# Index key and heads' weights of a sparse-attention indexer: two products or one of 80 columns

## The reference

```python
proj = h @ w_in[l]
q, k, v, ga, iq, ik, iw, xr, gr, ma, mb = jnp.split(proj, offsets, axis=-1)
iq = apply_rope(iq.reshape(B, S, 16, 64), cos_i, sin_i)   # index queries, 16 heads of 64
ik = apply_rope(ik, cos_i, sin_i)                         # one index key of 64
...
iw = iw.astype(jnp.float32) * (IDX_HEADS ** -0.5) * (IDX_DIM ** -0.5)   # one weight per head
dots = jnp.einsum('bqhd,bsd->bqhs', iqb, ik)
idx_score = jnp.einsum('bqh,bqhs->bqs', iwb, jax.nn.relu(dots))
```

## Time and profile before

| | |
|---|---|
| median of 3 runs | 2320.51 us (2318.68 to 2321.33) |
| the profiled execution | 2316.55 us, its span 2314.4 us |
| mean granted clock of the profiled execution | 0.985 |
| PE busy | 2206.8 us, 95% of the span |
| DVE busy | 1760.8 us, 76% |
| ACT busy | 1468.9 us, 63% |
| second block | from about 1540 us of the span to its end |
| heads' weights' products | 1613.5 us and 1985.1 us of the span |

### The profile page before, as it was taken

How to read it: one execution, slowest core, us unless ns; L and a number is a source line. 1 busy time by engine, 2 the same in 40 slices (tenths; PEclk the granted TensorE clock), 3 DMA queues, 4 the chain that set the end, 5 groups by cost and what they waited for, 6 DMA issues and landing times.

```text
span 2314.4 us, 35167 instructions
## 1 busy us (share of the span) xinstructions
PE 2206.8 (95%) x14207; PEld 1954.5 (84%) x14207; DVE 1760.8 (76%) x2214; ACT 1468.9 (63%) x1954; POOL 326.6 (14%) x314
## 2 busy tenths in 40 slices
PE   7789999988999999999999999969999999999998
PEld 7778999867888888888888888859898998989898
DVE  5634655788999999989898999964589666379865
ACT  5432444556877777777777878753575845466754
POOL 0510000000000000000000000003556200555500
PEclk9999999998999999999999999989999999999999
DMA  9522655517999999999999999946545365655452
GB/s 252 134 74 74 234 186 173 182 65 253 334 341 387 362 358 353 356 355 365 351 364 348 367 342 367 373 168 200 177 146 164 113 221 155 215 163 149 139 154 102
DMA packets 328401, 556.48 MB, mean 240 GB/s; under 512 B 23616, under 2 KB 164680, under 8 KB 328232
## 3 DMA queue, kind: packets, MB, share of 16 engines
q1 hardware_dynamic: 318432, 527.63, 65.6%
q0 software_dynamic: 9120, 25.97, 4.7%
q10 hardware_dynamic: 680, 0.54, 0.1%
HBM read 544.12 MB, written 9.96 MB: 239 GB/s over the span
## 4 chain that ended last, share of the span: by engine, by line
PE 77%; DVE 14%; ACT 6%; issue 3%; DMA 0%; SPq 0%; ACTq 0%; DVEq 0%
PE bank L856 23%; PE bank L858 22%; PE bank L857 22%; DVE parts L2435 4%; ACT parts L1806 2%; PE bank L862 1%; PE bank L1522 1%; DVE work L3189 1%; PE bank L1008 1%; DVE fast L2435 1%; PE bank L1583 1%; DVE work L3206 1%; DMA raw<-in_a_w_in_dram 0%; ACT work L2363 0%; PE bank L1730 0%
## 5 line engine op out<-in xcount | busy, mean ns | idle before, releaser
L2435 DVE TENSOR_TENSOR parts<-raw,parts 128x1024 fp32r<-128x1024 f32 (+1 forms) x713 | 858.3, 1219 | 385.9 <-ACT parts L1806 363.0
L1806 ACT CAST parts<-raw 128x1024 fp32r<-128x1024 f32 (+1 forms) x713 | 732.8, 1035 | 502.7 <-PE bank L858 486.7
L856 PE MATMUL bank<-cols,parts 128*128 128x256 f32 x1680 | 494.4, 294 | 8.9 <-DVE parts L2435 5.4
L858 PE MATMUL bank<-cols,parts 128*128 128x256 f32 x1680 | 479.1, 285 | 2.9 <-issue 2.9
L857 PE MATMUL bank<-cols,parts 128*128 128x256 f32 x1680 | 479.5, 285 | 0.0
L2435 DVE TENSOR_TENSOR fast<-raw,fast 128x1024 fp32r<-128x1024 f32 x302 | 362.0, 1219 | 32.0 <-ACT fast L1806 14.8
L1806 ACT CAST fast<-raw 128x1024 fp32r<-128x1024 f32 x302 | 315.8, 1052 | 95.0 <-PE bank L858 87.3
L856 PEld LDWEIGHTS bank<-cols,parts 128*128 128x128 f32 x1680 | 326.5, 194 | 22.5 <-issue 18.6
L857 PEld LDWEIGHTS bank<-cols,parts 128*128 128x128 f32 x1680 | 326.7, 194 | 4.9 <-issue 4.1
L858 PEld LDWEIGHTS bank<-cols,parts 128*128 128x128 f32 x1680 | 326.5, 194 | 0.0
L856 PE MATMUL bank<-parts,cols 128*128 128x512 f32 x740 | 295.1, 399 | 13.6 <-DVE parts L2435 6.9
(11 more groups left out here) (384 smaller groups left out, 3498.8 us busy)
## 6 DMA issues: line engine op xcount, KB each, us to landing
raw<-in_moe_w_gate_dram SPq DMA_DIRECT2D x112, 1024.0 KB, 7.4
raw<-in_moe_w_up_dram SPq DMA_DIRECT2D x112, 1024.0 KB, 7.1
raw<-in_moe_w_down_dram SPq DMA_DIRECT2D x112, 1024.0 KB, 7.2
raw<-in_w_in_dram SPq DMA_DIRECT2D x76, 1024.0 KB, 5.5
raw<-in_a_w_in_dram SPq DMA_DIRECT2D x12, 1024.0 KB, 12.3
raw<-in_ffn_w_gate_dram SPq DMA_DIRECT2D x11, 1024.0 KB, 5.2
raw<-in_ffn_w_up_dram SPq DMA_DIRECT2D x11, 1024.0 KB, 5.2
raw<-in_ffn_w_down_dram SPq DMA_DIRECT2D x11, 1024.0 KB, 4.9
```

The lines of the kernel that those rows point to most:

```text
L856: pe.matmul(o, l[0], r[0], start=start, stop=False)
L858: return pe.matmul(o, l[1], r[0], start=False, stop=stop)
L1806: a.copy(dst[0], src).then_inc(*up(o + "hi", x))
L2435: v.tensor_tensor(dst[1], src, dst[0].bitcast(F32), ALU.subtract).then_inc(*up(o + "lo", x))
```

## The change

Key and heads' weights become one chunk, one piece and one product of 80 columns (`ikw`), features on the partitions: key on 0 to 63, weights on 64 to 79. ACT copies the 80 x 256 result to `L2.ikw`, which lies in the relu buffer. In the indexer's first step PE multiplies the key half by the unit matrix and by the rotation matrix, each twice, for partitions 0 to 63 and 64 to 127 of bank 5 (fp32), which doubles and turns it; and it turns the weights to tokens on the partitions by two products with a 16 x 16 unit matrix into bank 4. ACT scales those into `L2.iwv` in its own first step of the indexer (after which bank 4 is free), DVE takes sine and cosine products from bank 5 and adds. The two halves of the weights' sum are no longer apart, so DVE's addition goes. The diff, without the lists of event names:

```diff
@@ layout
-    L2.iw2 = LD[:, 0, 0:64]
-    L2.iwv = v4(L2.iw2, 2, 2)[:, :, 0, :]
+    L2.iwv = v3(LD[:, 0, 0:32], 2)
...
+    L2.ikw = L2.rl[0:80, 1, 0:T]
@@ chunks and pieces
-        x, = W.chunk((8, 128), [(at_cols(64 * i, 64), wv[:, :, O_IK:O_IK + 64]) for i in range(2)], [whole])
-        W.used(x)
-        t["ik"] = x
-        t["iw"] = narrow_table(wv[:, :, O_IW:O_IW + 16], 16)
+        t["ikw"] = narrow_table(wv[:, :, O_IK:O_IW + 16], 80)
@@ PE, the indexer's first step
+                pe.wait_ge(*at("ikw", l))
+                claim(5)
+                for j, m in enumerate((ident, C(C_ROTI))):
+                    for rs in (slice(0, 64), slice(64, 128)):
+                        k = pe.matmul(bank[5][rs, j * T:(j + 1) * T], m[0:64, 0:64], L2.ikw[0:64, :], start=True, stop=True)
+                k.then_inc(*up("rot", l, "ik", 0))
+                busy[5] = ("ik_cos", l)
+                claim(4)
+                for t in range(2):
+                    k = pe.matmul(bank[4][:, 16 * t:16 * t + 16], L2.ikw[64:80, t * 128:(t + 1) * 128], ident[64:80, 64:80], start=True, stop=True)
+                k.then_inc(*up("iw_turned", l))
+                busy[4] = ("iw", l)
                 pe.wait_ge(*at("iq", l, 6))
-                yield from rope(L2.IK.unsqueeze(1), 1, C(C_ROTI), "ik", 1)
+                yield
                 yield from rope(L2.IQ, 8, C(C_ROTI), "iq")
@@ PE, the projection
-            x = t_["ik"]
+            x = t_["ikw"]
...
-                k_ = mm3(bank[4][:, 0:T], sl(w, ALL, k), sl(XT, ALL, k), k == 0, k == 7)
+                k_ = mm3(bank[4][0:80, 0:T], sl(w, ALL, k), sl(XT, ALL, k), k == 0, k == 7)
             k_.then_inc(*up("used", x))
-            narrow(bank[4][:, T:T + 64], t_["iw"], 16, 4)
-            busy[4] = ("iw", l)
+            busy[4] = ("ikw", l)
@@ ACT, the indexer's first step
+                a.wait_ge(*at("iw_turned", l))
+                a.mul(L2.iwv, v3(bank[4][:, 0:32], 2), 0.03125).then_inc(*up("iw", l))
@@ ACT, the projection
-            after(t_["ik"])
-            after(t_["iw"])
-            a.wait_ge(*at("used", t_["iw"]))
-            a.copy(L2.IK, bank[4][:, 0:T]).then_inc(*up("ik", l))
-            a.mul(L2.iw2, bank[4][:, T:T + 64], 0.03125).then_inc(*up("iw", l))
+            after(t_["ikw"])
+            a.wait_ge(*at("used", t_["ikw"]))
+            a.copy(L2.ikw, bank[4][0:80, 0:T]).then_inc(*up("ikw", l))
@@ DVE, the indexer
-                yield from rope(L2.IK.unsqueeze(1), 1, cosI, sinI, "ik", 1)
+                r_ = L2.rt[:, 1, 0:T]
+                v.wait_ge(*at("rot", l, "ik", 0))
+                v.tensor_tensor(r_, bank[5][:, T:2 * T], sinI, ALU.mult).then_inc(*up("rot_sin", l, "ik", 0))
+                v.tensor_tensor(L2.IK, bank[5][:, 0:T], cosI, ALU.mult).then_inc(*up("ik_cos", l))
+                v.wait_ge(*at("ik_cos", l))
+                v.tensor_tensor(L2.IK, L2.IK, r_, ALU.add).then_inc(*up("roped", l, "ik", 0))
+                v.wait_ge(*at("roped", l, "ik", 0))
+                yield
...
                 v.wait_ge(*at("iw", l))
-                v.tensor_tensor(L2.iwv, L2.iwv, v4(L2.iw2, 2, 2)[:, :, 1, :], ALU.add).then_inc(*up("dve"))
-                v.wait_ge(*at("dve"))
```

More of the change, by code:

```diff
@@ L43 @@
     "pe_attention": ("scores", "p_turned", "pv"),
-    "pe_index": ("rot", "dots"),
+    "pe_index": ("rot", "iw_turned", "dots"),
     "pe_route": ("counts", "two_turned"),
@@ L57 @@
     "act_attention": ("exps", "pT", "probs_a"),
-    "act_index": ("iw", "ik", "relu"),
+    "act_index": ("iw", "ikw", "relu"),
     "act_columns": ("iq", "xr", "q", "k", "v", "ga_th", "gr_th", "ma", "mb"),
@@ L73 @@
     "dve_setup": ("two_rows", "lam_min", "angle", "co_angle"),
-    "dve_index": ("rot_sin", "roped", "weighed", "kept"),
+    "dve_index": ("rot_sin", "ik_cos", "roped", "weighed", "kept"),
     "pool_gdn": ("level", "k_beta", "q_dec", "k_dec", "z_scaled"),
```

## The result

The kernel after takes 2307.78 us (median of 5 runs, 2305.24 to 2310.21) against 2320.51 us; the ratio is 0.9948, 95% interval 0.9937 to 0.9959, which is 12.1 us. Two later timings of the same kernel gave 0.9963 (0.9951 to 0.9976) and 0.9957 (0.9944 to 0.9970); the mean of the three, 0.9956, is 10.2 us. The sign was right, the size was not.

A forecast was written before the change was run, and what follows sets the result against it. PE was taken to bound the kernel. Per layer 3.58 - 1.8 = 1.8 us, two layers 3.6, with the clock's 3.0 a gain of 6.6: 2313.9 us, range 2309.5 to 2318.5.

The forecast's parts named there:

- What bounds the kernel: Second block's first layer: PE, busy 69.60 of 70 us from 1570 to 1640; a step earlier there moves the chain earlier.
- rival C: From 1640 on DVE is the bound and hides PE's gain; 0 to 3 us gained, 2317.5 to 2320.5; chance 0.12.
- The first layer's key product to iq's first: Place of the heads' weights' 32 narrow products on PE; removing them was to save 3.58 us per layer.
- The index step and its wait: Indexer's first step: 1.28 us extra on PE, then 0.5 us waiting for ACT's scaling before iq's first rotation; slip 1.8.
- rival E: In the index step pairs don't overlap and turning drains: slip 2.6, sum 5.0, 2315.5 us; within the forecast's 0.42.
- the bounds 0 and 0.2: Gain in us from the 24 key products having 80 weight columns for 128; 0 was taken.
- At nothing: Fewer casts and loads, the key's evacuation, DVE's dropped addition and bank 5 held longer: all covered, counted as zero time.
- So I count 3.0 once: Half clock during the second layer's narrow products, 6.8 us long: one fall, 3.0 us regained in total.
- I put the same difference on it: The median lay 4 us above the profiled execution; the same difference was added to 2309.9, giving 2313.9 us.
- rival B: Both layers lose their clock fall in the typical run: 3.6 + 6.0 = 9.6 us, 2310.9 us; chance 0.15.
- Rival A: The clock's fall at the narrow products stays or moves elsewhere: only 3.6 us gained, 2316.9 us; chance 0.24.
- rival D: The clock falls in the new index step in both layers, long enough to make the kernel slower: 2326 us; chance 0.07.

The follow-up runs named there:

- the early variants: Kernel after with the key's and weights' small products, ACT's scaling and DVE's key rotation moved behind iq's second pair; ratio 0.9950, with ACT key copies 0.9945 and 0.9944.
- the wide and narrow fillers: Kernel after with 3.6 us a layer of unused products put back at the old place, of 256 columns (2315.95 us) or of 32 and 16 (2321.9 us).
- The two later profiles: The kernel before, unchanged, profiled again and a third time; 2319.95 us and, in one run, 2318.63 us.

## Why the prediction was wrong

*What bounds the kernel* held: each step taken off PE before v1 came out behind it, and rival C (hidden) fell. The first layer's key product to iq's first: 3.58 us were forecast, and the first recurrent products came 3.7 us earlier (86.3 to 82.6, both without a fall, 0.07 of it from the narrower weight loads).

*The index step and its wait* held: 1.28 and 0.5 us were forecast, 1.3 and 0.54 came, and from the recurrent block's first products to the dots it is 30.8 us against 29.0: 1.8, as forecast. Pairs of column halves overlap: the two records of a pair start 6 ns apart, the pairs 0.21 to 0.27 us; rival E fell. The 24 key products at 80 columns gained 0.07 us, inside the bounds 0 and 0.2. The page of the Trainium skill (TensorE: Matmul & The Clock Gate, section LDWEIGHTS) is right that the load itself is shorter with fewer columns (148 ns against 192 in this profile), but the step from product to product went only from 0.12 to 0.117, so its 0.26 us did not come.

*At nothing*: fewer loads and casts showed nothing on the way to the recurrent block, by the table's first columns. DVE's key rotation was counted as hidden; the early variants show that it is worth 0.6 us in DVE's full stretch (PE's wait before the dots, 1.19 against 1.78 us), but that is no part of the change, which left it where it was.

*The step that failed* is the clock's: "So I count 3.0 once: what the profiled execution lost to it", together with "I put the same difference on it" for the median. The price was right: 3.1 us per fall (the forecast's own numbers give 6.8 - 4.0 = 2.8 and 3.0 where it wrote 2.9 to 3.1; it took 3.0). The count was not. I took the falls of one execution for those of every execution, and the 4 us between its time and the median for something that both kernels share. The two later profiles, with both falls, have a block of 764.2 and 763.7 us against 760.6, so the missing second fall fits most of those 4 us. Two falls make 3.6 + 6.2 = 9.8 us, rival B (9.6), to which I gave 0.15; the mean of the three timings is 10.2, of which some 0.3 lies outside the span, and the means of the three blocks differ by 9.8 (762.8 and 753.0). The rows in hand spoke for it: three places with such products, two falls, and a profiled run that is faster than every timed one. Rival A (the fall is not theirs) fell by the wide and narrow fillers. The Trainium skill's advice against gaps (the same page, section Why this matters for your kernels) is no full account here: at the narrow places of the fillers PE is busy without a gap before and in both falls.

*Slower* (rival D) fell: the clock is 1.00 in the index step in all three executions of after.

*What stays open.* The first ratio is 2 us beyond the 9.8. Luck fits it: the mean granted clock of its five runs is 0.986, and 0.984 to 0.985 in the eleven later ones, which were slower by 2.5 us in the mean. The other falls behind v1 are six in three executions of before and three in three of after. Those at the first dots cost 1.4 us, those at the start of a layer 1.5 to 1.6, and those near 1760 at most 0.3. The ones at the dots have another look than those of the narrow products: each begins within 1.7 us after PE's wait of 1.8 us for DVE. They came in 8 of 20 such places, and in none of six in the early variants, where the wait is 1.2 us; six are too few to show that the shorter wait avoids them. Whether the change makes other falls rarer, or three executions are too few, was not tried.

## What to carry to other kernels

Price a run of narrow products by more than its time: 32 in a row cost 3.6 us of PE and, in seven of eight places, 3.1 us more behind them at half clock, while the same number spread between wide ones, or the same time in wide ones, cost no fall. A fall of the clock that one profile shows at a place is a chance at each like place and not a count; where the profiled run is faster than the median, ask which falls it was spared, and compare the mean granted clock of the timed runs. Lengths from a mark in the same execution tell 0.1 us where medians of whole runs tell 2.

## What the runs showed of the hardware

The clock fell to 0.50 with PE busy at 100%, 2.3 to 3.1 us after the first of 32 products of 32 and 16 columns, so while these still ran, and stayed there for 6.8 us although wide products followed at once. Pairs of plain fp32 products on the same rows and different column halves overlap fully: eight records of 64 x 64 by 256 in 1.08 us, the two of a pair 6 ns apart. ACT copied 64 x 256 elements from partitions 0 to 63 to partitions 64 to 127 in 0.365 us, against 0.359 to the same partitions.
